# Splitting two of four raw value units, and moving the sample group's steps one unit later, in a two-layer decoder step on one core

## What is computed

```python
q, k, v, qi, ki, wi = jnp.split(a @ w_in, ATTN_SPLITS, axis=-1)   # a: rmsnorm of the 264 tokens, 1024 wide
score = einsum(relu(qi . ki), wi) * IDX_SCALE                     # the indexer: 4 heads of 64
_, idx = lax.top_k(score, 64)                                     # 64 keys for each query
# prompt: softmax over the picked keys of q . k, times v (8 heads of 128)
# sample: the 64 picked rows of the paged caches are gathered: cache_k[idx], cache_v[idx]
logits = einsum('bqhd,bqkhd->bqhk', q, k_sel) * HEAD_DIM ** -0.5
o = einsum('bqhk,bqkhd->bqhd', softmax(logits), v_sel)
```

## Time and profile before

| | us |
|---|---|
| median of three runs | 592.01 |
| lowest and highest | 591.72, 592.43 |
| the profiled execution, its device time | 592.18 |
| its span from the first to the last instruction | 590.4 |
| PE busy | 579.4 (98%) |
| DVE, ACT, POOL busy | 453.6 (77%), 369.7 (63%), 226.8 (38%) |

### The profile page before, as it was taken

How to read it: one execution, slowest core, us unless ns; L and a number is a source line. 1 busy time by engine, 2 the same in 40 slices (tenths; PEclk the granted TensorE clock), 3 DMA queues, 4 the chain that set the end, 5 groups by cost and what they waited for, 6 DMA issues and landing times.

```text
span 590.4 us, 12747 instructions
## 1 busy us (share of the span) xinstructions
PE 579.4 (98%) x5015; PEld 502.8 (85%) x5015; DVE 453.6 (77%) x904; ACT 369.7 (63%) x629; POOL 226.8 (38%) x230
## 2 busy tenths in 40 slices
PE   7999999999999999999999999999999999999995
PEld 7888889888888888888888888888888888888885
DVE  4899996666897778787778898789878777885542
ACT  6985566676765666575555788856756566654322
POOL 4241466713354544551000112273644555432220
PEclk9999999999999999999999999999999999999998
DMA  9959694329766766678997952065766666879602
GB/s 264 263 137 278 184 339 133 108 80 324 209 200 194 198 195 195 197 226 244 259 264 216 239 170 73 1 179 172 207 193 199 192 195 199 233 220 240 175 7 74
DMA packets 205420, 113.28 MB, mean 192 GB/s; under 512 B 5561, under 2 KB 202217, under 8 KB 205337
## 3 DMA queue, kind: packets, MB, share of 16 engines
q1 hardware_dynamic: 203169, 106.33, 63.9%
q0 software_dynamic: 1680, 5.79, 2.8%
q10 hardware_dynamic: 512, 0.35, 0.2%
HBM read 108.83 MB, written 3.86 MB: 191 GB/s over the span
## 4 chain that ended last, share of the span: by engine, by line
PE 92%; DVE 3%; POOL 1%; ACT 1%; issue 1%; DVEq 0%; ACTq 0%; POOLq 0%
PE acc L1538 25%; PE acc L1535 25%; PE acc L1541 25%; PE acc L1506 2%; PE acc L1726 1%; PE acc L1728 1%; PE acc L1727 1%; PE misc L1897 1%; PE acc L1561 1%; DVE w_lo L997 1%; PE misc L1663 1%; POOL hT L1930 1%; ACT w_hi L593 1%; PE misc L1642 1%; PE misc L1626 1%
## 5 line engine op out<-in xcount | busy, mean ns | idle before, releaser
L1535 PE MATMUL acc<-aH,w_hi 128*128 128x264 f16 (+1 forms) x886 | 244.5, 276 | 0.8 <-DVE work L1310 0.7
L1538 PE MATMUL acc<-aL,w_hi 128*128 128x264 f16 (+1 forms) x886 | 244.5, 276 | 0.0
L1541 PE MATMUL acc<-aH,w_lo 128*128 128x264 f16 (+1 forms) x886 | 244.5, 276 | 0.0
L997 DVE SCALAR_TENSOR_TENSOR w_lo<-stage,w_hi 128x1024 f16<-128x1024 f32 (+1 forms) x155 | 205.7, 1332 | 30.4 <-ACT w_hi L593 29.9
L593 ACT ACTIVATE w_hi<-stage 128x1024 f16<-128x1024 f32 (+1 forms) x155 | 171.1, 1109 | 32.4 <-PE acc L1541 25.2
L1535 PE MATMUL acc<-zH,w_hi 128*128 128x264 f16 x384 | 106.0, 276 | 0.0
L1538 PE MATMUL acc<-zL,w_hi 128*128 128x264 f16 x384 | 106.0, 276 | 0.0
L1541 PE MATMUL acc<-zH,w_lo 128*128 128x264 f16 x384 | 106.0, 276 | 0.0
L1538 PEld LDWEIGHTS acc<-aL,w_hi 128*128 128x128 f16 (+1 forms) x886 | 88.1, 99 | 13.5
L1535 PEld LDWEIGHTS acc<-aH,w_hi 128*128 128x128 f16 (+1 forms) x886 | 86.8, 98 | 14.5 <-issue 1.5
L1541 PEld LDWEIGHTS acc<-aH,w_lo 128*128 128x128 f16 (+1 forms) x886 | 88.1, 99 | 12.6
(11 more groups left out here) (421 smaller groups left out, 951.7 us busy)
## 6 DMA issues: line engine op xcount, KB each, us to landing
stage<-in_w_ffn_up SPq DMA_DIRECT2D x88, 512.0 KB, 4.7
stage<-in_w_ffn_down SPq DMA_DIRECT2D x32, 704.0 KB, 5.7
stage<-in_w_attn_in SPq DMA_DIRECT2D x22, 512.0 KB, 6.6
stage<-in_w_rec_in SPq DMA_DIRECT2D x16, 512.0 KB, 4.9
stage<-in_w_attn_out SPq DMA_DIRECT2D x8, 512.0 KB, 3.8
stage<-in_w_rec_out SPq DMA_DIRECT2D x8, 512.0 KB, 3.8
area<-in_w_attn_in SPq DMA_DIRECT2D x4, 512.0 KB, 4.6
area<-in_x_prompt SPq DMA_DIRECT2D x2, 512.0 KB, 4.6
```

The costliest lines, as they stand in the source:

```text
L997: v.scalar_tensor_tensor(low, stage[:, place_in_line(u) % 4, 0:n, 0:cols], WSCALE, high, ALU.mult, ALU.subtract).then_inc(lo_done, 1)
L1535: t_.matmul(out, high[:, c, :], xH[:, x0 + c, :], start=first and c == 0, stop=False)
L1538: t_.matmul(out, high[:, c, :], xL[:, x0 + c, :], start=False, stop=False)
L1541: ins = t_.matmul(out, low[:, c, :], xH[:, x0 + c, :], start=False, stop=last and c == n - 1)
```

## The change

`RAW_V` shrinks from units 13 to 16 to units 15 and 16. Units 13 and 14 are split like all others, in steps 9 and 10, and loaded through `stage`; the two loads of raw weights that stay are issued behind them. On PE `turn_picked` moves from unit 14 into unit 15, behind `spread_queries`. The four `sample_dots` stand in steps 16 to 19 in place of 15, 16, 16 and 17; the turn of their results, the maxima, the exponential, `turn_weights`, `pb` and the two units with `sample_values` each come one step later (the value products lie now in units 24 and 25).

```diff
--- before.py
+++ after.py
@@ -63,7 +63,7 @@
 OWN_HOME = [*range(U_OUT + SLOTS, U_OUT + DC), *range(U_XB, U_XB + EARLY), *range(U_XB + EARLY + SLOTS, U_ROUT + SLOTS)]
 
 
-RAW_V = U_V[2:6]
+RAW_V = U_V[4:6]
 SPLIT_AT = {u: u - SLOTS for u in range(SLOTS, U_OUT + SLOTS) if u not in RAW_V}
 
 
@@ -800,7 +800,7 @@
                     after_heads(u)
                 if u < U_OUT and u not in U_V:
                     swap_halves(u)
-                if u == 21:
+                if u == 22:
                     act.wait_ge(smx_done, 1)
                     nc.scalar.activation(sl[:], sl[:], ACT.Exp).then_inc(sexp_done, 1)
                 if u == INSIDE + 1:
@@ -1151,7 +1151,7 @@
                 if u == 3:
                     dve.wait_ge(roped, 3)
                     v.tensor_copy(kiT[ID:P, :], kiT[0:ID, :]).then_inc(ki_twice, 1)
-                if u == 22:
+                if u == 23:
                     dve.wait_ge(sp_turned, 1)
                     v.tensor_tensor(pb[:].rearrange("p j h s -> p (j h) s"), E[:, 0:32].unsqueeze(2).to_broadcast([P, 32, NS]),
                                     own[:].unsqueeze(1).to_broadcast([P, 32, NS]), ALU.mult)
@@ -1208,8 +1208,8 @@
                     dve.wait_ge(so_hi, 1)
                     dve.wait_ge(so_done, 1)
                     v.tensor_tensor(zL[:, 0:H, TP:T], by_head(onw2[:]), zH[:, 0:H, TP:T], ALU.subtract).then_inc(o_lo, 1)
-                if 15 <= u < 17:
-                    sample_dots(u - 15)
+                if u == 16:
+                    sample_dots(0)
                 if u != INSIDE:
                     for x in splits_of_step(u):
                         lo(x)
@@ -1241,9 +1241,9 @@
                     take_merged(6, 1)
                     rope(12)
                     take_merged(7, 1, found=True)
-                if 16 <= u < 18:
-                    sample_dots(u - 14)
-                if u == 20:
+                if 17 <= u < 20:
+                    sample_dots(u - 16)
+                if u == 21:
 
                     dve.wait_ge(sl_turned, 1)
                     past = E[0:NS, :]
@@ -1752,17 +1752,15 @@
                 if u == 3:
                     pe.wait_ge(x_kept, 2)
                 if u < U_OUT:
-                    if u in (23, 24):
-                        between = lambda i: sample_values(4 * (u - 23) + i // 4, i % 4)
+                    if u in (24, 25):
+                        between = lambda i: sample_values(4 * (u - 24) + i // 4, i % 4)
                     elif u == 5:
                         between = lambda i: index_products() if i == 6 else None
                     elif u == 6:
                         between = lambda i: late_scores() if i == 4 else None
-                    elif u == 14:
-                        between = lambda i: turn_picked() if i == 8 else None
                     elif u == 15:
-                        between = lambda i: spread_queries() if i == 4 else None
-                    elif u == 22:
+                        between = lambda i: spread_queries() if i == 4 else turn_picked() if i == 8 else None
+                    elif u == 23:
                         between = lambda i: turn_weights() if i == 8 else None
                     elif u == INSIDE:
                         between = lambda i: heads_of_step(INSIDE) if i == 7 else None
```

## The result

The changed kernel takes **601.26 us**, the median of six runs from 599.14 to 602.93; the kernel before, run beside it, takes 592.15 (591.72 to 592.68). The ratio is 1.0152, 95% interval 1.0127 to 1.0177. The direction was as predicted, the size was not: +9.1 us where +3.65 was forecast, and outside the range. Lines from 1755 on stand two lower than before: L1815 is now L1813, L2020 is L2018, L2046 is L2044.

A forecast was written before the change was run, and what follows sets the result against it. PE, busy 98% of the span, was taken as the bound. Terms -1.74 + 2.84 + 1.6 + 0.6 + 0.6 - 0.25 = +3.65 on the profiled 592.18, less 0.17 to the median, gave 595.6 us; range 592.8 to 597.9.

The forecast's parts named there:

- The gain of two units, -1.74: On PE, units 13 and 14 split take 2.70 us each instead of 3.57 raw: 0.87 less per unit.
- DVE's delay and the first wait, +2.84: Two new lo ahead of rope(12) make DVE 3.55 us late; PE waits 2.84 at v2's turn for ACT's L715.
- The loads: Stage places for units 21 to 25 free 3.5 to 5 us later; loads of 6.6 us still arrive in time, cost nothing.
- The second wait, for the dots, +1.6: PE at L1815 behind unit 21 waits for DVE's last dots, ready at 91.9; +1.6 us, bounds 0.5 and 2.2.
- The rule of the Trainium skill, "SBUF — State Buffer", "Who interferes with whom": DVE and POOL exclude each other for whole instructions, so three rotations cost: dots 0.6 later, at 92.5, time 596.2.
- Softmax and weights, +0.6 and +0.6 less 0.25: PE waits at L1716 for the exponential, +0.6, and for turn_p(0) and pb, +0.6; the small mb wait goes, -0.25.
- The -0.25: PE's small wait for mb at 94.65 in the kernel before was to disappear, saving 0.25 us.
- My upper bound of +5.9: All terms at their upper bounds together: +5.9 us, a time of 597.9.
- The clock, a rival at 0.09: PE's clock halves in the new 2.84 us wait, slowing unit 15: 598.0 to 600.5; chance 0.09.
- one of my signs of being wrong: The prediction counts as wrong if the granted clock drops in the stretch.
- The rule that I cited from the Trainium skill, "TensorE: Matmul & The Clock Gate", Part 1: An idle PE falls to half clock until busy again; speaks against changes that put such a gap into PE.
- My price of 2.4 to 4.9: Clock rival's cost: +4.9 us if unit 15 with its contents, 4.87 us, ran wholly at half speed, +2.4 if half.

The follow-up runs named there:

- x2_steps_only: Changed kernel with its four raw units back, so that only the sample steps are moved one unit later; 599.01 us, ratio 1.0117.
- x3_keep_first: Changed kernel with ACT in step 13 keeping the turned v1 and v2 ahead of the query copies; 598.14 us.
- y1_pause: Changed kernel with POOL's value gathers held until PE's unit 17 is done instead of unit 16; 600.68 us.
- y2_steps_pause: Sample steps moved alone, four raw units, with the value gathers held until unit 17 is done; 598.93 us.
- y3_first_pause: Changed kernel with ACT keeping v1 and v2 ahead of step 13's query copies and value gathers held until unit 17 is done; 598.42 us.
- u1_rows_early_warm: Changed kernel, row numbers turned after unit 15's second piece, first wait filled with 11 matmuls of ones; 598.33 us.
- u2_first_rows_early: Changed kernel, ACT keeping v1 and v2 ahead of step 13's query copies, row numbers turned after unit 15's fourth piece; 598.58 us.
- w2_last_two_split: Kernel before with units 15 and 16 split instead, lo(15) behind the search, lo(16) to lo(18) behind the index; 595.74 us, ratio 1.0061.
- z1_rows_back: Sample steps moved alone, four raw units, with only the row numbers' turn put back inside unit 14; 596.12 us, ratio 1.0068.
- z4_rows_early: Changed kernel with row numbers turned after unit 15's second piece instead of its fifth, query spreading behind it; 600.17 us.
- v2_keys_held: Sample steps moved alone, four raw units, row numbers' turn back in unit 14, key gathers held until unit 15 is done; 597.45 us, ratio 1.0084.
- x4_lo_first: Changed kernel with DVE in step 14 doing lo(18) ahead of the index, in its idle time; 598.73 us.
- y4_warm: Changed kernel with matmuls of ones into an unused bank in both PE waits, 11 in step 14, 15 in step 20; 599.85 us.

## Why the prediction was right and wrong

- **The gain of two units, -1.74: right.** PE was at the turn of v2 at 65.16 - 2.59 = 62.57 by the modelled end of its last matmul, at 62.40 by start times; 62.57 was computed.
- **DVE's delay and the first wait, +2.84: right**, 2.59 (2.76 by start times), for the instruction named and through L778, at 63.34 for 63.6.
- **The loads, "in my sums each still lands at least 1.5 us ahead of its `hi`, so nothing": wrong, and the step that failed.** I priced a load at 6.6 us, the median of the whole program. Two loads stood behind the moved turn on DVE and beside the moved gathers, and took 10.3 and 12.6. Cost: 3.43 of wait and 1.66 of clock in the profiled run. I wrote what a late `hi` would cost and did not check the DMA share of the stretch, 1.01. The load on which PE's wait hangs is that of unit 23: before, it landed at 72.9 + 6.1 = 79.0, 4.7 us ahead of `hi(23)` at 83.7; it is now issued 3.2 later, takes 6.5 longer, and ACT asks for it 1.8 later (88.71 - 3.16 = 85.55): 4.7 - 3.2 - 6.5 + 1.8 = -3.2, the 3.16 of the row. At 6.6 us it would have landed at 82.7, 2.9 ahead. For unit 22: before, the load landed at 67.9 + 8.5 = 76.4, 3.8 us ahead of `hi(22)` at 80.2; it is now issued 5.2 later, takes 1.8 longer, and ACT asks for it only 0.9 later (83.44 - 2.38 = 81.06): 3.8 - 5.2 - 1.8 + 0.9 = -2.3, the 2.38 of the row. At 6.6 us it would have landed at 79.7, 1.4 ahead: the instants behind my margin of 1.5 were right, the landing times were not. The 8.5 us that this same load took before the change, which its trace held, would have told of a load 0.5 late. The eight profiles in which PE waits at the turn of k1 with the load of unit 22 behind the first gather (the changed kernel, `x2_steps_only`, `x3_keep_first`, `y1_pause`, `y2_steps_pause`, `y3_first_pause`, `u1_rows_early_warm`, `u2_first_rows_early`) have that turn 19.5 to 21.1 us after the first key gather; `w2_last_two_split`, with a like wait and the load at 68.3, has it at 22.8.
- **The second wait, for the dots, +1.6: right as a mechanism, absent from the result.** 1.23 in `z1_rows_back`, `z4_rows_early` and one of two executions of `v2_keys_held`; in the changed kernel the loads hold PE longer. The rule of the Trainium skill, "SBUF — State Buffer", "Who interferes with whom", would have made the dots 0.6 later. The lengthening itself is seen at each of three rotations in `z1_rows_back` (0.82, 0.56 and 0.55 us on DVE, below), the longer wait is not.
- **Softmax and weights, +0.6 and +0.6 less 0.25: too much.** With the dots in their place 0.39, 0.35 and 0.41; in the changed kernel 0.41 and 0.30. The -0.25 did not come: ahead of the first value product PE's starts are 0.34 us apart (105.15 to 105.49), before 0.21 (94.44 to 94.65). My upper bound of +5.9 had left it out; with it the sum is +5.65.
- **The clock, a rival at 0.09: its mechanism holds**, and a drop of the clock was one of my signs of being wrong. It fell in the second wait of the changed kernel, and in the first wait of two profiles (`x4_lo_first`, `z4_rows_early`), not in that of two others (the changed kernel, `y1_pause`), with the same 2.6 us of idle time. Whether it also did so in the slower ones of the six runs is open: `y4_warm` gained 1.4 us, but those runs have no profile. The rule that I cited from the Trainium skill, "TensorE: Matmul & The Clock Gate", Part 1, agrees with the rows behind the wait of 3.43 us (0.63 and 0.52), not with those behind two of the four waits of 2.6, where the clock stayed at 1.00. My price of 2.4 to 4.9 was mostly too high: 1.76 in `z4_rows_early` for the first wait; for the second 1.5 to 2.8, since from the turn of k1 to that of k2 PE takes 2.9 us without a loss, 4.4 in `x3_keep_first` and 5.7 in `u2_first_rows_early`.
- **That the whole is no sum.** PE's gains ahead of step 20 come back in part as wait there: of -2.4 us in `x3_keep_first` 1.2 did. I treated each wait as added to the ones before.

## What to carry to other kernels

When a change moves a large DMA, or the release of one, look at the DMA share of the stretch in which it lands. If it is full, take a load's price from the loads of that stretch (8.5 and 6.1 us here before the change, 10.3 and 12.6 after it), not from its median over the program, and look which load lands last ahead of the engine that needs it. Where PE waits for such a backlog, savings ahead of it are handed back in part. Of the 15 waits of 2.5 us or more in these profiles all but two were followed by microseconds at half clock; price the pair.

## What was not expected of the hardware

- A load of 512 KB by SP took 3.6 to 4.2 us when it was issued with no gather and no other load in flight, 4.5 with one load ahead of it (`x4_lo_first`), and up to 15.4 beside gathers. Loads alone lengthen each other as well: the four issued from 49.0 to 53.3 in the kernel before, behind the four raw loads (44.6 to 47.8) and with no gather in flight, took 6.1 to 8.5. How much of the 10.3 and 12.6 is due to the gathers and how much to the neighbouring loads no run separates. The issue itself stretches too: 368 ns in most cases, 3994 ns at 81.0 in the changed kernel.
- Each of three rotations on POOL lengthens what runs beside it on DVE, and two of the three take longer themselves. DVE and POOL of `z1_rows_back`; L1136 (a dot product) takes 0.28 otherwise, L997 (`lo`) 1.22, L2046 (the rotation) 0.74:

```profile
78.29 2.04 DVE L997 SCALAR_TENSOR_TENSOR w_lo<-stage,w_hi 128x1024 f16<-128x1024 f32 x1 [0.30 <-ACT w_hi L593]
84.02 0.84 DVE L1136 CUSTOM_DVE_ANT_0 area<-area 128x128 f32<-128x128 f32 x1
88.35 0.83 DVE L1136 CUSTOM_DVE_ANT_0 area<-area 128x128 f32<-128x128 f32 x1
```

```profile
78.48 0.76 POOL L2046 TENSOR_TENSOR area<-area,scratch 128x264 f32<-128x264 f32 x1
83.05 1.66 POOL L2046 TENSOR_TENSOR area<-area,scratch 128x264 f32<-128x264 f32 x1 [3.81 <-DVE area L1081]
87.38 1.65 POOL L2046 TENSOR_TENSOR area<-area,scratch 128x264 f32<-128x264 f32 x1 [2.66 <-DVE area L1081]
```

- Idle times of PE of the same length (2.57 to 2.59 us, same place, same work ahead) were followed by the full clock in two profiles and by half clock in two. What decides stayed open.
